# T1 of the MLP weight chains by accumulating transfer, copies out of PSUM between the halves of a weight split, T3's sums side by side, and later first turns

## The reference

```python
h = rmsnorm(x, g[2])
f = jnp.square(jax.nn.relu(h @ mlp_w1[i])) @ mlp_w2[i]
x = x + rmsnorm(f, g[3])
```

## Time and profile before

| what | value |
|---|---|
| median of three runs | 2310.95 us |
| the profiled execution's own time | 2310.16 us |
| its span | 2308.4 us |
| PE busy, matmuls | 2271.1 us (98%), 10609 |
| DVE busy | 1718.6 us (74%) |
| ACT busy | 1316.3 us (57%) |
| DVE sums `R_f<-R_f,X` (T1), 128 x 2048 | 28 |
| accumulating transfers `R_f<-in_w_u`, POOL | 56 |
| granted clock, mean | 0.996 |

### The profile page before, as it was taken

How to read it: one execution, slowest core, us unless ns; L and a number is a source line. 1 busy time by engine, 2 the same in 40 slices (tenths; PEclk the granted TensorE clock), 3 DMA queues, 4 the chain that set the end, 5 groups by cost and what they waited for, 6 DMA issues and landing times.

```text
span 2308.4 us, 26572 instructions
## 1 busy us (share of the span) xinstructions
PE 2271.1 (98%) x10609; PEld 1874.3 (81%) x10609; DVE 1718.6 (74%) x2043; ACT 1316.3 (57%) x1769; POOL 80.9 (4%) x110
## 2 busy tenths in 40 slices
PE   9999999999999999999999999999999999999998
PEld 7778788878888878888887888888888888888887
DVE  6575864888788888887878888878878775456664
ACT  6444444756665656656665666656655564444453
POOL 0000000000000000000000000000000010000000
PEclk9999999999999999999999999999999999999999
DMA  9445455777787687787575786786796745654343
GB/s 350 165 149 183 161 182 183 273 211 257 252 265 249 242 249 243 247 252 266 219 289 151 272 269 194 284 273 185 274 288 182 270 163 196 253 186 147 147 151 123
DMA packets 73099, 513.26 MB, mean 222 GB/s; under 512 B 8233, under 2 KB 8564, under 8 KB 13519
## 3 DMA queue, kind: packets, MB, share of 16 engines
q1 hardware_dynamic: 61568, 429.58, 49.3%
q0 software_dynamic: 11264, 81.87, 15.8%
q10 hardware_dynamic: 144, 0.12, 0.0%
HBM read 505.24 MB, written 6.29 MB: 222 GB/s over the span
## 4 chain that ended last, share of the span: by engine, by line
PE 77%; DVE 13%; DMA 5%; ACT 3%; issue 1%; POOL 0%; ACTq 0%; POOLq 0%; DVEq 0%
PE P L353 74%; DVE low L616 8%; DMA raw<-in_w_d 5%; PE P L356 3%; ACT hi L497 2%; DVE R_m L601 1%; DVE X L601 1%; DVE EV L601 1%; ACT EV L553 1%; DVE R_f L601 0%; ACT R_h L492 0%; DVE R_f_r L601 0%; DVE R_h L604 0%; DVE X L604 0%; DVE R_h L601 0%
## 5 line engine op out<-in xcount | busy, mean ns | idle before, releaser
L616 DVE TENSOR_TENSOR low<-raw,hi 128x1024 fp32r<-128x1024 f32 (+3 forms) x694 | 810.3, 1201 | 376.7 <-ACT hi L497 373.7
L497 ACT ACTIVATE hi<-raw 128x1024 fp32r<-128x1024 f32 (+3 forms) x694 | 702.0, 1040 | 490.3 <-PE P L353 335.8
L353 PE MATMUL P<-hi,R_h 128*128 128x512 f32 (+2 forms) x2944 | 948.5, 394 | 0.8 <-DVE R_h L604 0.4
L353 PE MATMUL P<-hi,R_f_r 128*128 128x512 f32 x2480 | 797.7, 394 | 21.4 <-DVE R_m L601 12.9
L353 PEld LDWEIGHTS P<-hi,R_h 128*128 128x128 f32 x2944 | 552.5, 188 | 118.2 <-issue 8.1
L353 PE MATMUL P<-low,R_h 128*128 128x512 f32 (+2 forms) x1472 | 570.7, 388 | 0.0
L353 PEld LDWEIGHTS P<-hi,R_f_r 128*128 128x128 f32 x2480 | 468.6, 189 | 125.8 <-DVE low L616 27.7
L353 PE MATMUL P<-low,R_f_r 128*128 128x512 f32 x1240 | 485.4, 391 | 0.0
L353 PEld LDWEIGHTS P<-low,R_h 128*128 128x128 f32 x1472 | 276.9, 188 | 56.6 <-issue 4.6
L616 DVE TENSOR_TENSOR low<-R_f,hi 128x1024 fp32r<-128x1024 f32 x226 | 261.8, 1220 | 31.3 <-ACT hi L497 31.3
L353 PEld LDWEIGHTS P<-low,R_f_r 128*128 128x128 f32 x1240 | 234.5, 189 | 47.0
(11 more groups left out here) (221 smaller groups left out, 1457.3 us busy)
## 6 DMA issues: line engine op xcount, KB each, us to landing
raw<-in_w_d SPq DMA_DIRECT2D x128, 1024.0 KB, 7.5
raw<-in_w_u SPq DMA_DIRECT2D x72, 1024.0 KB, 5.4
R_f<-in_w_u POOLq DMA_DIRECT2D x56, 1024.0 KB, 10.3
raw<-in_w_z SPq DMA_DIRECT2D x45, 1024.0 KB, 4.8
raw<-in_w_i SPq DMA_DIRECT2D x36, 1024.0 KB, 4.8
R_f<-in_w_u SPq DMA_DIRECT2D x28, 1024.0 KB, 9.1
X<-in_w_u SPq DMA_DIRECT2D x28, 1024.0 KB, 9.8
raw<-in_w_mo SPq DMA_DIRECT2D x16, 1024.0 KB, 4.9
```

The source lines that it names most:

```text
L353: return self.e.matmul(o, l, r, start=start, stop=stop, skip_group_check=True)
L497: self.e.activation(hi, raw, ACT.Copy).then_inc(*self.inc("high_made", ("high", k, d)))
L616: self.e.tensor_tensor(low, raw, hi.bitcast(f32), ALU.subtract).then_inc(*self.inc("low_made", *lows))
```

## The change

T1's additions become transfers too, so that POOL issues 84 accumulating transfers and DVE has 28 sums less. `split_ahead` and `release` take a function `between` that is called between the two halves of the first split tile, and the copies out of PSUM after an up product (`end`) and after a down pair (`summed`) are given to it. Both sums of `third_sum` stand in the middle of d2. In the first mixer, four empty entries in place of two stand ahead of the first group's turns and one in place of none ahead of the second's.

```diff
     def link(mlp_, e, s, j, free):
         w = a[f"w_u{mlp_}"]
-        if s == 0:
-            return
-        if s in (1, 2):
+        if s < 3:
             E.chain_add(j, m.chain[j], w[8 * e + CHAIN[s + 1] + j], free, ("chained", mlp_, e, s + 1, j))
...
-    def split_ahead(n):
+    def split_ahead(n, between=None):
...
                 split_part(k, 0, 2)
+                if between is not None:
+                    between()
+                    between = None
                 split_part(k, 1, 2)
             at_["high"] += 1
+        if between is not None:
+            between()
...
-        later += [nop] * {0: 2, 8: 1, 9: 1, 10: 1}.get(n, 0)
+        later += [nop] * {0: 4, 1: 1, 8: 1, 9: 1, 10: 1}.get(n, 0)
...
-                if n == 1 and soon:
-                    end(b, ("product", j, 1))
-                release(j, ("product", j, 1))
-                if n == 1 and not soon:
-                    end(b, ("product", j, 1))
+                done = "product", j, 1
+                release(j, done, between=(lambda: end(b, done)) if n == 1 else None)
...
-            release(j, done)
-            if q == 1:
-                for t in range(2):
-                    summed(e, t, g, banks[t], done)
+            release(j, done, between=(lambda: [summed(e, t, g, banks[t], done) for t in range(2)]) if q == 1 else None)
...
-            down(0, lambda: first_sum(0))
-            up(2, 0, HH[:, HRIGHT, TOP], HL[:, HRIGHT, TOP], h_right, plain(b21), second, onto=ms[1], aside=lambda: first_sum(1))
+            down(0)
+            up(2, 0, HH[:, HRIGHT, TOP], HL[:, HRIGHT, TOP], h_right, plain(b21), second, onto=ms[1])
...
-            down(2, lambda: third_sum(0))
+            down(2, lambda: [third_sum(j) for j in range(2)])
```

More of the change, by code:

```diff
@@ L1119, in split_ahead @@
                 if o >= NO and o - NO not in used:
-                    return
+                    break
                 split_part(k, 0, 2)
+                if between is not None:
+                    between()
+                    between = None
                 split_part(k, 1, 2)
             at_["high"] += 1
+        if between is not None:
+            between()
     def quarters():
@@ L1156, in take, with release @@
         return j, m.hi[o % NO][0:parts, 0:c], m.low[o % NO][0:parts, 0:c]
-    def release(j, done, hold=False):
+    def release(j, done, hold=False, between=None):
         l, o = plan[j][6:8]
@@ L1165, in release @@
         if not hold:
-            split_ahead(j + 2 + AHEAD)
+            split_ahead(j + 2 + AHEAD, between)
     bank_free, bank_held = [[] for _ in range(8)], set()
@@ L1859, in parts_of, with half_product @@
             s_m[n] = plain_parts(SH[n], SL[n], SUM[n], [s_m[n], list(free)])
-        def half_product(b, xh, xl, ready, tiles, end, soon, onto, aside):
+        def half_product(b, xh, xl, ready, tiles, end, onto, aside):
             for n, tile in enumerate(tiles):
@@ L1872, in half_product @@
                               onto is None and n == k == 0, n == 1 and k == 3, x, bank_free[b], *whose)
-                if n == 1 and soon:
-                    end(b, ("product", j, 1))
-                release(j, ("product", j, 1))
-                if n == 1 and not soon:
-                    end(b, ("product", j, 1))
+                done = "product", j, 1
+                release(j, done, between=(lambda: end(b, done)) if n == 1 else None)
                 step()
-            return ("product", j, 1)
+            return done
         def down_tile(e, i, banks, middle):
@@ L1957, in both_ways @@
             kept_at = at_["take"] + 9
-            def first_sum(j):
-                E.tile_sum(m.chain[j], m.chain[j + 2], [("chained", l, e, 0, j), ("linked", l, e, j)], ("chained", l, e, 1, j))
             def third_sum(j):
@@ L1972, in both_ways, with up @@
             up_done = {}
-            def up(n, b, xh, xl, ready, tiles, end, soon=False, onto=None, aside=nop):
-                up_done[n] = half_product(up_banks[b], xh, xl, ready, tiles, end, soon, onto, aside)
+            def up(n, b, xh, xl, ready, tiles, end, onto=None, aside=nop):
+                up_done[n] = half_product(up_banks[b], xh, xl, ready, tiles, end, onto, aside)
             def down(i, middle=nop):
@@ L1983, in both_ways @@
             up(1, 0, HH[:, HLEFT, TOP], HL[:, HLEFT, TOP], h_left, linked(0), first)
-            down(0, lambda: first_sum(0))
-            up(2, 0, HH[:, HRIGHT, TOP], HL[:, HRIGHT, TOP], h_right, plain(b21), second, onto=ms[1], aside=lambda: first_sum(1))
+            down(0)
+            up(2, 0, HH[:, HRIGHT, TOP], HL[:, HRIGHT, TOP], h_right, plain(b21), second, onto=ms[1])
             down(1)
             up(5, 1, SH[1], SL[1], s_m[1], linked(1), fifth)
-            down(2, lambda: third_sum(0))
+            down(2, lambda: [third_sum(j) for j in range(2)])
             up(3, 1, SH[4], SL[4], s_m[4], plain(b22, "kept"), third, onto=ms[5])
             down(3)
-            up(6, 0, SH[2], SL[2], s_m[2], linked(2), sixth, True, aside=lambda: third_sum(1))
+            up(6, 0, SH[2], SL[2], s_m[2], linked(2), sixth)
             down(4)
@@ L1994, in both_ways @@
             down(5)
-            up(4, 1, HH[:, HRIGHT, BOTTOM], HL[:, HRIGHT, BOTTOM], h_right, linked(3), fourth, True)
+            up(4, 1, HH[:, HRIGHT, BOTTOM], HL[:, HRIGHT, BOTTOM], h_right, linked(3), fourth)
             left_free = down(6)
```

## The result

The changed kernel takes 2275.2 us (median of four runs, 2273.95 to 2275.38) against 2310.7 us for the kernel before beside it (2309.43 to 2312.64): a ratio of 0.9843, 95% interval 0.9828 to 0.9859. The profiled execution took 2275.38 us with a span of 2273.5, against 2310.16 and 2308.4.

A forecast was written before the change was run, and what follows sets the result against it. PE, with an instruction in flight in 98% of the span, was taken as the bound. Terms 14.5 + 12 + 1.5 + 3 - 1 - 0.5 = 29.5 us off 2310.16 gave 2280.7, forecast 2281, range 2276 to 2297.

The forecast's parts named there:

- With every wait gone it would be 2277: Whole kernel: all counted waits removed, 33.2 us off the profiled execution's 2310.16 us.
- d6, 12 waits: d6 in steps 2 to 7, both layers: waits for DVE's sums into `R_m` go, 14.5 us (bounds 13.6 to 14.7).
- 12 x 0.15 of refilling: At d6: 0.15 us lost per wait besides 12.9 us idle, 14.7 us in all.
- first steps, 2: d3 of step 1, both layers: 3.65 us wait and slow-clock matmuls behind it go, 12 us (bounds 0 to 13.0).
- smaller waits: Four other PE waits for a `low` tile with their refilling: 1.5 us won, bounds 0 to 2.2.
- start: First turns: two PE waits for ACT's `EV` are covered by later turns, 3 us won, bounds 0 and 3.3.
- transfers, third sum's load: Costs in the steps: 1 us for added accumulating transfers delaying d1, 0.5 us for d3's later load.
- bounds of the term: by the order alone: At d6: the new order of DVE's queue by itself wins 1.13 x 12 = 13.6 us.
- rival that its wait stays: d3 of step 1: its transfer stays late, 12 us are not won, 2293 us; chance 0.13.
- They fit, barely: DMA at 705 to 725 us: two new transfers want 11 us where 11.65 us are free.
- slow rival: New transfers make d1's load late, 3 us a step, 42 us of wait, 2323 us; chance 0.07.
- the DMA gives some back: d1 or d3 starts up to 1 us late in each of 14 steps, 2295 us; chance 0.13.

The follow-up runs named there:

- order alone: The kernel before with only the copies out of PSUM put between the halves of a split: 2297.4 us, ratio 0.9939.
- seven a step: The changed kernel with the first of T3's two sums as an accumulating transfer too, seven per step: 2290.8 us, ratio 0.9912.
- eight transfers: The changed kernel with both of T3's sums as accumulating transfers too, eight per step: 2315.3 us, ratio 1.0018.
- late third sum: The changed kernel with the second sum of `third_sum` behind up 6's first tile again: 2290.0 us, ratio 0.9887.
- late idle instruction: The changed kernel plus a DVE instruction behind up 6's first tile that only reads as much as a sum: 2281.1 us, ratio 0.9873.

## Why the prediction was nearly right, and where it failed

**What failed in the time is the size of the sum.** The mechanisms that it counts are there; what each part was credited with is another matter (d6, below). "With every wait gone it would be 2277" was the floor, and 29.5 of its 33.2 us were taken. All waits did go, and they were worth more:

| term | taken | measured | why |
|---|---|---|---|
| d6, 12 waits | 14.5 | 16.0 | starts late by 14.8 in all, plus 0.1 behind each; "12 x 0.15 of refilling" on top of the idle time covered only the late starts |
| first steps, 2 | 12 | 13.6 | nothing stayed: 7.15 + 7.27, less 2 x 0.42 for the little `low` wait behind up 6 |
| smaller waits | 1.5 | 3.4 | the rest of the MLP's 33.0 (32.1 of MLP time, and 0.9 for d6 of the last step, which lies behind its end); nothing stayed |
| start | 3 | 3.1 | the first up 5 at 473.09 instead of 476.18; without the turns' edit it is at 475.35, so the turns are 2.3 of it and the rest is within what the start varies by |
| transfers, third sum's load | -1.5 | 0 | no wait of PE |

The sum is 36.1 us; the profiled executions differ by 34.8, because the changed one ran part of a stretch behind the MLP at the lower clock (0.66 in the last window above). Its second profiled execution has 1.00 there and a span of 2272.5, 35.9 us less than before. The 0.8 us that the forecast added from the profiled execution to the median did not come back either: now the median is 0.2 us below that execution. The step of mine that failed is thus the deduction: I took 3.7 us off the floor for leftovers and a DMA price, each a piece of a range and none read from a row, and the idle time plus 0.15 us undersized the floor by another 2.9. The low end of 2276 lay 1 us under a floor that was itself too high.

**d6.** The mechanism as predicted is shown: order alone leaves d6 0.34 us late in step 3, 0.17 of it shown as idle, and 0 to 0.35 in the twelve steps (the count said 0.15 to 0.3). But "bounds of the term: by the order alone" gave the order 13.6 of the 14.7 us, as if the parts added up. Alone they give 10.7 (order), 19.3 (third sum) and 13.9 us (T1) of MLP time, 43.9 together, and all of them 32.1 (by the runs 13.5, 22.1 and 15.4 against 35.5 with the turns). Taken away from the whole they cost about 1, 14 and 12. The order and the third sum cure the same wait, and the third sum, which I gave 1.1 us and a subordinate clause, also keeps the loads from bunching.

**The first step.** Right in each link: T1's sums delay the issue by 2 to 2.5 us and the data by 4.5. The rival that its wait stays is refuted by both kernels with T1 alone and without it.

**The DMA.** "They fit, barely" is what the valley shows; a transfer costs 5.3 us of the engines (43.1 us for 8.51 MB) and a plain one 2.65. The slow rival was a real one, one transfer away: with seven a step, d3 is late, with eight the gain is gone. And "the DMA gives some back" at 2295 would have been about the truth had the third sum not moved: that kernel is at 2290.

**DVE's busy time** fell by 50.7 us (1718.6 to 1667.9) and not by 64. DVE's groups by form, before and then after:

```profile
L616 DVE TENSOR_TENSOR low<-R_f,hi 128x1024 fp32r<-128x1024 f32 x226 | 261.8, 1220 | 31.3 <-ACT hi L497 31.3
```
```profile
L616 DVE TENSOR_TENSOR low<-R_f,hi 128x1024 fp32r<-128x1024 f32 x226 | 267.4, 1220 | 82.8 <-ACT hi L497 82.3
```

An instruction that follows another directly overlaps it in the records by 0.09 us (two halves of 1.22 show 2.35). With more gaps there is less overlap, and the same 226 halves show as 5.6 us more; the halves from `raw` and `X` add 5.5 in the same way (784.5 to 787.8 and 66.0 to 68.2). The last 2 us of the 13 are not traced.

**POOL's issues.** 84 of them now take 849, 865 and 912 ns at least, in the middle and at most, as the 56 did in the earlier trace rows. The prediction set this against a rule of the Trainium skill ("SBUF — State Buffer", Who interferes with whom) and applied it too widely. That section of the Trainium skill says of `tensor_tensor` that it has no two-port mode, the mode in which DVE locks GpSimd out, and DVE's splits and sums here are of that kind. The trace agrees: no issue is longer. What an instruction of the locking kind would do here no run shows.

## What to carry to other kernels

Where several edits shorten one chain of an engine, ask of each wait how many of them cure it; one kernel with each part alone and one without it tell apart what adds up. Of an operation that moves, price also the buffer it holds and the ordered loads behind that buffer: here the place of one 2.28 us sum moved the issue of three loads by 5 to 18 us and the time by 14 us. And when every wait that feeds a tight pipeline goes, expect the sum of late starts plus about 0.1 us each, and take leftovers off only where a row shows one.

## What the runs showed of the hardware

- Accumulating transfers take twice a plain one's time on the engines (5.3 and 2.65 us a megabyte tile). PE has no wait in the steps at a DMA share of 0.92, 13 waits at 0.96 and 25 at 0.97 to 0.98 (with the open end named above).
- Matmuls 0.43 us apart (the lower clock) followed starts that were 3.65 us late, 2.6 us (the order alone, layer 1) and 3.4 us (eight transfers), and none in the steps that were late by 1.91 us or less. Of four that were late by 1.96 to 2.2 us two were followed by them (late third sum, late idle instruction, both in layer 0) and two not. And one long wait cost nothing besides: in the kernel with the order alone d3 of step 1, layer 1, starts 3.56 us late, and the clock stays up (PE's timeline and a window, columns as in the earlier trace rows):

```profile
1258.09 0.50 PE L353 MATMUL P<-hi,R_f_r 128*128 128x512 f32 x1 [3.41 <-DVE low L616]
```
```profile
1258.00:1264.00 6.00, 5.91 (x26) 4.91 (x27) 6.00 (x7) 4.61 (x6) 0.86 (x1) 1.00 0.22 23
```

The length of a single wait thus does not decide it by itself. "TensorE: Matmul & The Clock Gate" (HAM oscillation) of the Trainium skill says that such a gap can cost a second time; these runs agree that it can, and show that at 2 us, and once at 3.6, it need not.
